# One weight buffer more in a decoder trunk on one core: three 2 MB loads fewer, and an expert ring of eight rows, then of ten

## What is computed

```python
def peer(h, wq, subkeys, u_tab, v_tab):
    q = (xt @ wq).reshape(t, PEER_HEADS, 2, PEER_HALF)
    sc = jnp.einsum('thpc,pkc->thpk', q, subkeys, preferred_element_type=jnp.float32)
    sv, si = lax.top_k(sc, PEER_TOPK)
    cand = sv[:, :, 0, :, None] + sv[:, :, 1, None, :]
    ...
    cs, cpos = lax.top_k(cand.reshape(t, PEER_HEADS, -1), PEER_TOPK)
    idx = jnp.take_along_axis(cidx.reshape(t, PEER_HEADS, -1), cpos, axis=-1)
    gate = jax.nn.softmax(cs, axis=-1)
    ...
        act = jax.nn.gelu(jnp.einsum('td,tkd->tk', xbb, u_tab[ib], preferred_element_type=jnp.float32))
        return jnp.einsum('tk,tkd->td', gb * act, v_tab[ib].astype(jnp.float32))
```

## Time and profile before

| | |
|---|---|
| time, median of 3 executions | 1553.74 us (1551.52 to 1554.93) |
| time of the profiled execution | 1553.37 us |
| its span, first to last instruction | 1551.6 us |
| TensorE busy | 71% |
| VectorE busy | 72% |
| ScalarE busy | 50% |
| GpSimd busy | 38% |
| bytes moved by DMA | 603.39 MB, 389 GB/s over the span |
| share of the 16 DMA engines: gathers, other loads | 84.8%, 11.3% |

### The profile page before, as it was taken

One profiled execution on the slowest core, in us unless ns is written; L12 is line 12 of the kernel. 1 busy time (PEld: TensorE's weight loads), 2 busy tenths in 40 slices (PEclk: granted clock), 3 DMA queues, 4 the chain that ended last, 5 costly groups with the idle time before them and its releaser, 6 DMA issues.

```text
span 1551.6 us, 19133 instructions
## 1 busy us (share of the span) xinstructions
PE 1097.8 (71%) x5920; PEld 348.4 (22%) x5920; DVE 1111.5 (72%) x2533; ACT 770.2 (50%) x2120; POOL 589.4 (38%) x517
## 2 busy tenths in 40 slices
PE   7997678866765666679866575656878666666665
PEld 3542222322211212223221121212323111111110
DVE  2356887479787899985477799999456866666554
ACT  2315554445456667764334666766334644444433
POOL 0024343323443354554334345344432443434430
PEclk9998689878966776879988567686998777676675
DMA  9569999999999998999999999999999999999995
GB/s 358 179 234 413 420 405 418 414 415 408 415 421 421 354 374 358 410 421 415 412 413 414 403 357 369 355 363 406 380 416 415 415 422 421 421 421 421 421 422 234
DMA packets 105418, 603.39 MB, mean 389 GB/s; under 512 B 9314, under 2 KB 9442, under 8 KB 39780
## 3 DMA queue, kind: packets, MB, share of 16 engines
q0 software_dynamic: 73728, 536.90, 84.8%
q1 hardware_dynamic: 31588, 65.26, 11.3%
HBM read 601.08 MB, written 1.05 MB: 388 GB/s over the span
## 4 chain that ended last, share of the span: by engine, by line
DMA 32%; DVE 31%; PE 22%; ACT 7%; issue 3%; DVEq 3%; ACTq 1%; POOL 1%; SPq 0%; POOLq 0%
DMA rings<-in_uv_tab_dram,idx 24%; DVE rings L1324 11%; PE ps L715 9%; PE ps L920 8%; DMA wst<-in_wq_dram 7%; DVE mem L1231 2%; PE ps L908 2%; DVE dgs L1324 2%; ACT dgs L667 1%; DVE mem L1213 1%; ACT wgt L664 1%; DMA rings<-in_w_in_dram 1%; DVE mem L1242 1%; ACT L661 1%; DVE mem L1240 1%
## 5 line engine op out<-in xcount | busy, mean ns | idle before, releaser
L920 PE MATMUL ps<-rings,dgs 64*64 64x512 f32 x3648 | 638.0, 804 | 343.3 <-ACT dgs L667 342.6
L463 POOL DMA_INDIRECT rings<-in_uv_tab_dram,idx x456 | 521.7, 1144 | 804.3 <-PE ps L920 687.8
L1324 DVE CUSTOM_DVE_ANT_0 rings<-rings,h 128x1024 f32<-128x1024 f32 x456 | 550.7, 1224 | 210.8 <-DMA rings<-in_uv_tab_dram,idx 197.7
L661 ACT ACTIVATE gel<-dots 128x1 f32<-128x1 f32 x512 | 102.1, 199 | 522.2 <-DVE dots L1324 518.5
L920 PEld LDWEIGHTS ps<-rings,dgs 64*64 64x64 f32 x3648 | 128.3, 163 | 783.4 <-ACT dgs L667 682.3
L667 ACT ACTIVATE dgs<-cst,wgt 128x128 f32<-128x128 f32 x512 | 205.6, 402 | 36.3 <-issue 1.5
L715 PE MATMUL ps<-wst,hT 128*128 128x512 f32 x320 | 168.0, 666 | 37.1 <-DMA wst<-in_wq_dram 20.5
L664 ACT ACTIVATE wgt<-gel,share 128x1 f32<-128x1 f32 x512 | 150.8, 295 | 35.5 <-issue 0.3
L920 PE MATMUL ps<-dgs 64*64 64x512 f32 x448 | 80.2, 795 | 53.2 <-ACT dgs L667 53.1
L463 POOL DMA_INDIRECT dgs<-in_uv_tab_dram,idx x56 | 65.9, 1176 | 88.3 <-PE ps L920 74.8
L715 PEld LDWEIGHTS ps<-wst,hT 128*128 128x128 f32 x320 | 63.4, 212 | 138.1 <-issue 134.9
(11 more groups left out here) (192 smaller groups left out, 991.2 us busy)
## 6 DMA issues: line engine op xcount, KB each, us to landing
wst<-in_wq_dram SPq DMA_DIRECT2D x15, 2048.0 KB, 28.2
wst<-in_w_out_dram SPq DMA_DIRECT2D x4, 2048.0 KB, 22.8
wst<-in_glu_w_dram SPq DMA_DIRECT2D x4, 2048.0 KB, 31.7
rings<-in_uv_tab_dram,idx POOLq DMA_INDIRECT x456, 15.7
rings<-in_w_in_dram SPq DMA_DIRECT2D x3, 2048.0 KB, 16.7
rings<-in_w_in_dram SPq DMA_DIRECT2D x2, 1024.0 KB, 7.5
dgs<-in_w_in_dram SPq DMA_DIRECT2D x1, 2048.0 KB, 19.4
vec<-in_vecs_dram SPq DMA_DIRECT2D x3, 512.0 KB, 17.2
```

Source lines behind the costliest of these rows:

```text
L463: nc.gpsimd.indirect_dma_start(out=ring[g % RING], out_offset=None, in_=uv_tab, in_offset=bass.IndirectOffsetOnAxis(ap=idx[n % AHEAD][:, s ...
L661: A.activation(gel[i][:, every], dots[i][:, every], ACT.Gelu_apprx_tanh)
L920: ins = PE.matmul(ps[64 * b:64 * b + 64, 4 + 2 * t + half, :], diag[rows, g % DIAGS, rows], ring[g % RING][rows, D + b * BANK:D + (b + 1) ...
L1324: V.tensor_tensor_reduce(out=u, in0=u, in1=h[:, t, :], scale=1.0, scalar=0.0, op0=ALU.mult, op1=ALU.add, accum_out=dots[n % 2][:, s:s + 1] ...
```

## The change

- A third weight buffer: the whole tile `dgs` (2 MB), free once block 3 of the input projection has been used for both tiles. For that (1, 3) moves ahead to the first place of tile 1 in `Z_ORDER`.
- The output projection's two blocks stay in the halves of `wst` from their use for tile 0 (uses 0 and 1) to that for tile 1 (uses 5 and 6). Query blocks 0, 1 and 2 of layer 0 pass one after the other through the third buffer; block 2 stays there until its use for tile 1 (use 9). `BLOCK_OF` names the block of each use, `BUFFER` the buffer of each block. There are 20 loads.
- The diagonals move to a tile of their own (`dia`), 7 slots instead of 16, and ScalarE waits for the row that had the slot.
- The ring has 8 slots (all in `rings`) for rows 0 to 79 and 10 from row 80 on (two more in `dgs`, once use 9 is over). The copies of indices and gates go from 16 to 8.
- The queries of tile 1 come in the order 3, 2, 0, 1, at slots 68, 74, 81, 89 instead of 3, 0, 1, 2 at 68, 76, 84, 92; the routing of groups 6 to 12 starts 4 to 6 slots later.

```diff
-RING = 9
-AHEAD = 16
+SHORT, RING = 8, 10
+SHORT_ROWS = 80
+AHEAD = 8
 PACE = 1
-DIAGS = 16
+DIAGS = 7
...
-SHARED_USE = 8
+BLOCK_OF = [0, 1, 2, 3, 4, 0, 1, 5, 5, 4, 6, 7] + list(range(8, 20))
+BUFFER = [0, 1, 2, 2, 2, 0, 1, 0] + [1, 0] * 6
...
-Z_ORDER = [(0, 0), (0, 1), (0, 2), (0, 4), (0, 3), (1, 0), (1, 1), (1, 2), (1, 4), (1, 3)]
+Z_ORDER = [(0, 0), (0, 1), (0, 2), (0, 4), (0, 3), (1, 3), (1, 0), (1, 1), (1, 2), (1, 4)]
...
             def load_w(*which):
                 for w in which:
-                    if w >= 2:
-                        last_use = w - 2 + (w - 2 >= SHARED_USE - 1)
+                    earlier = [v for v in range(w) if BUFFER[v] == BUFFER[w]]
+                    if earlier:
+                        last_use = max(u for u in range(len(BLOCK_OF)) if BLOCK_OF[u] == earlier[-1])
                         sp.wait_ge(w_used, last_use + 1)
+                    elif BUFFER[w] == 2:
+                        sp.wait_ge(z_done, Z_ORDER.index((1, 3)) + 1)
...
-                if g < RING and g % 2 == 0:
-                    pool.wait_ge(z_done, 6 + g // 2)
-                if g >= RING:
-                    pool.wait_ge(v_done, g - RING + 1)
+                if g < SHORT and g % 2 == 0:
+                    pool.wait_ge(z_done, 7 + g // 2)
+                if row_ahead(g) >= 0:
+                    pool.wait_ge(v_done, row_ahead(g) + 1)
+                elif ring_at(g) == SHORT:
+                    pool.wait_ge(w_used, Q_USE[1, 2] + 1)
...
+                if g >= DIAGS:
+                    act.wait_ge(v_done, g - DIAGS + 1)
```

More of the change, by code:

```diff
@@ L154, in between @@
         at(0, slot, (names[0],))
-    query(0, 76, 1, 0)
-    query(0, 84, 1, 1)
-    query(0, 92, 1, 2)
+    query(5, 1, 1, 0)
+    query(5, 9, 1, 1)
     for t in range(T):
@@ L272, in trunk @@
         sgb = sb("sgb", [P, 8])
-        ring = [rings[:, 2 * D * i:2 * D * (i + 1)] for i in range(8)] + [dgs[:, 2 * D:4 * D]]
+        ring = [w[:, 2 * D * i:2 * D * (i + 1)] for w, rows in ((rings, SHORT), (dgs, RING - SHORT)) for i in range(rows)]
+        weights_in = [wst[:, 0, :, :], wst[:, 1, :, :], dgs[:, :].rearrange("p (k n) -> p k n", k=KC)]
         qs = part(8448, BANK)
@@ L317, in trunk @@
         ld_win = [sem(f"ld_win{n}") for n in range(5)]
-        ld_w = [sem(f"ld_w{i}") for i in range(2)]
+        ld_w = [sem(f"ld_w{i}") for i in range(3)]
         ld_vec, ld_col, ld_row = sem("ld_vec"), sem("ld_col"), sem("ld_row")
@@ L359, in bc, with ring_at, ring_turn, row_ahead @@
             return ap.to_broadcast([ap.shape[0]] + [ap.shape[1 + at] if d is None else d for d in dims])
+        def ring_at(g):
+            return g % SHORT if g < SHORT_ROWS else (g - SHORT_ROWS) % RING
+        def ring_turn(g):
+            b = ring_at(g)
+            return sum(ring_at(r) == b for r in range(g + 1))
+        def row_ahead(g):
+            earlier = [r for r in range(g) if ring_at(r) == ring_at(g)]
+            return earlier[-1] if earlier else -1
+        def nth_in(w):
+            return sum(BUFFER[i] == BUFFER[w] for i in range(w + 1))
         def block_of(use):
-            return use - (use >= SHARED_USE)
+            return BLOCK_OF[use]
         def score_cols(p, b):
-            c = 2 * (b if p == 0 else (b + 1) % 4)
+            c = 2 * ((2, 3, 1, 0)[b] if p == 1 else b)
             return slice(c, c + 2)
@@ L562, in q_keep @@
                 if p > 0:
-                    last = cols.stop if p == 1 else PH * (p - 1) + 2 * b + 2
+                    last = {1: cols.stop, 2: 2 * PH, 3: 2 * PH + cols.stop}[p]
                     act.wait_ge(idx_ok, last)
```

50 lines of the change are left out of this document (26 added, 24 removed).

## The result

| | before | changed |
|---|---|---|
| median of 19 runs (lowest to highest) | 1553.74 us (1551.52 to 1556.14) | 1559.84 us (1555.83 to 1561.77) |
| profiled execution, own time / span | 1553.37 / 1551.6 us | 1559.49 / 1557.8 us |
| bytes moved | 603.39 MB | 597.09 MB |

The ratio is 1.0035 [1.0028, 1.0042], paired by chip: 5.4 us slower (4.4 to 6.5). The forecast of 1548.0 has the wrong sign, and 1559.8 lies above its range. In what follows a ratio is turned into microseconds with 1553.9.

The account below looks back on a forecast made before the run. The prediction took the kernel as a prelude bound by its chain of operations, then alternating DMA-bound and VectorE-bound stages. Its terms, 5.8 + 1.9 - 10.0 + 1.8 - 5.0 = -5.5 us, gave 1548 us, range 1543 to 1555.

Parts of the forecast that it names:

- late first query load, and the clock behind it: Prelude: TensorE waits for the first query block, +5.8 us, then runs at half clock, +1.9 us; nothing covers the wait.
- two loads fewer: DMA-bound windows up to 510 us: two weight loads at 4.98 us each saved, -10.0 us; bounds 0 and -11.3.
- ring of eight for 80 rows: First 80 rows: gathers go out one row's completion later, +1.8 us, priced at row 37; bounds 0 and 4.6.
- then one slot more: Ring of ten from row 80: 2.49 us gained at the end of each of two VectorE-bound stages, -5.0 us.
- its own sign: Sign of being wrong: row 128 late by more than 3 us would fault the price of the loads or ring of eight.
- theory D: Theory set up for the experiments: the loads, once gone, bring nothing.
- the slow rival: VectorE, not DMA, sets the pace of rows 16 to 96, so the -10.0 falls away: +4.5 us, 1558; chance 0.10.
- the rival's 7.1: Ring of eight costs 7.1 instead of 1.8 us: feedback at every thin place plus a further row; 1553.3, chance 0.12.
- The rest at nothing: Diagonals, second block's rotary work, and moved queries and routings cost 0; the latter were said to stay in DMA-bound windows.
- My own sign: Sign of being right: row 128 nearly unchanged (-0.5 us), then -2.5 us at the end of each VectorE-bound stage.

Follow-up runs that it names:

- e7: Kernel before, with the first query block's load held until the sixth projection product is done: 1561.49 us, ratio 1.0051, +7.9 us.
- e5: Kernel before, with the output projection load issued at 203.68 us cut to an eighth of its bytes: 1549.67 us, ratio 0.9969, -4.8 us.
- e6: Kernel before, with the load issued at 341.5 us (query block 2, tile 1) cut to an eighth of its bytes: 1551.15 us, ratio 0.9985, -2.3 us.
- e3: Kernel before, with a ring of eight for rows 0 to 79, then nine: 1558.33 us, ratio 1.0032, +5.0 us.
- e10: Kernel before, with seven diagonals in their own tile and a ring of nine to row 80, then ten: 1548.47 us, ratio 0.9972, -4.4 us.
- e8: Kernel before, with only the routing of group 12 moved from slot 120 to 126: 1559.64 us, ratio 1.0036, +5.6 us.
- e1: Changed kernel, with routings of groups 8 to 12 moved earlier, group 12 from slot 126 to 120: 1555.66 us, ratio 1.0012 to the kernel before.
- e4: Kernel before with its 23 loads, seven diagonals in their own tile and a ring of ten from the first row: 1547.94 us, ratio 0.9961, -6.1 us.

## Why the prediction was wrong

The parts, each measured by itself at the kernel before, against the term that I gave them:

| part | forecast | measured | from |
|---|---|---|---|
| late first query load, and the clock behind it | +7.7 | +7.9 | e7 |
| two loads fewer | -10.0 | -8.2 | e5 and e6, times 8/7 |
| ring of eight for 80 rows | +1.8 | +5.0 | e3 |
| then one slot more | -5.0 | -4.4 | e10 |
| the rest: routing of group 12 past row 128 | 0 | +5.6 | e8 |
| sum | -5.5 | +5.9 | the kernel itself: +5.4 |

The sum of the parts lies within the interval of the whole, 4.4 to 6.5. Each part is known to about 2 us only, and their sum to about 5, so parts that were left out, or that act on each other, by less than that would not be seen here.

The rows of the changed kernel give a second account that does not need the parts to be independent. From one execution, it is 7.7 us at the first row (forecast 7.7), then +3.8 by row 16 (the ring of eight, 1.8), -4.9 between rows 16 and 128 (the two loads, -10.0), +5.8 between 128 and 136 (nothing), and -6.3 behind (the ring of ten, -5.0). Both accounts give the step at row 128 5.6 to 5.8 us. They differ on the ring of eight and the loads: 5.0 us worse than forecast by the parts, 7.1 by the rows. So the prediction also failed ahead of row 128, as its own sign says: from the first row to row 128 the changed kernel is 1.1 us shorter and not 8.2.

1. **The prelude** was right in each step: the issue after the projection piece (77.13, forecast 77.7), 8 us to landing, a wait of 5.72, and 1.82 us for the clock. That the idle stretch at 354 us with its half clock would repeat itself here was a good reading: the same length of idle, nearly the same price. Nothing behind the first gather takes it back (e7).

2. **The loads** were right in kind: theory D and the slow rival, by which the bytes bring nothing, fall with e5. The second was mis-sized, 2.7 instead of 5. Together with what else changes up to row 128 the changed kernel shows -4.9 where I had -10.0. The window 340 to 510 us has a DMA share of 1.01 as a whole, but the stretch behind the load, rows 80 to 104, gains nothing (e6), and only half of the load's time comes out at row 112. That the work of VectorE and TensorE for tile 1's queries keeps the rest back is what the place suggests; no run took that work away, so the cause of this half stays open. The Trainium skill, DMA: Bandwidth & Descriptors, section "Where 436 GB/s comes from", puts the memory's side at about 358 GB/s; by that figure 7/8 of a load is an estimated 5.1 us, by the 421 GB/s of the trace 4.4. The 4.8 measured (3.0 to 6.7) does not decide between them, but the changed kernel's 421 GB/s over 1300 to 1500 us does, and it does not agree with that section's figure. This program runs on one core alone, and no run here had a second core at work.

3. **The ring of eight** is a term that was mis-sized. I looked at the thinnest place of the trace, row 37, and said of it that "the delay does not feed back into the next issue". The first thin place was row 15. The trace of before has its issue 1.6 us ahead of a weight load, behind a query product; I costed the first rows only up to the seventh. There the ring of eight lets row 15 out behind the product and behind the load, 3.8 us of waiting at once (e3), of which 2.9 stay, and at rows 38 to 45 the delay does feed back while the load of 206 us runs beside them. The measured 5.0 (3.0 to 6.8) lies just above my upper bound of 4.6 and below the rival's 7.1; I had taken 1.8 from row 37 alone.

4. **The ring of ten** came as forecast in size (-4.4, interval -6.1 to -2.6), but not where. I had put -2.5 at the end of each VectorE-bound stage; in e10 the first gave -2.5 at row 232, lost again at row 248 and back at row 272, and the end of the second, between rows 336 and 360, near -4.4 more, of which the end kept all but some 0.2. That is -7.0 in an execution 2.1 us faster than its median, so the places are surer than the sizes.

5. **"The rest at nothing" is the step that failed.** I wrote that "the queries and routings that move by some slots stay in DMA-bound windows". For group 12 that is false: slot 126 plus the eight slots of a routing is 134, and from row 128 on gathers do not set the pace. I had read the whole window 340 to 510 us as DMA-bound by its share of 1.01. Row 128 is taken at 478.9 us in the kernel before and row 134 at 497.1, inside that window, where the share is still 1.01 but VectorE hardly waits for gathers. My own sign spoke of row 128 as the end of the stage; my price went by the window. I checked that the indices come early enough for their rows, which is a question of lateness, and not whether VectorE has waits for gathers to spare where the work lands, which is one of price. Six slots cost 5.6 us (3.4 to 7.8), the largest cost behind the prelude's 7.9, and as much as my whole forecast gain. In place of nothing the runs show 2.9 + 2.8 us of routing work on VectorE behind row 128 (e8), and a step that is gone when the routing ends at slot 128 again (e1). None of my rivals named it; the one that ended on the slow side was another mechanism, and it was false.

Of the 11.4 us between my sum and the sum of the parts, 5.6 are this step, 3.2 the ring, 1.8 the loads, 0.6 the ring of ten and 0.2 the prelude, each by its middle value. That the prelude and the ring of ten came out near their terms did not help: without the step of group 12, the parts still add up to about no change (+0.3), not to the forecast gain.

Open stays why group 12 alone costs 5.6 at the kernel before (e8) while moving it back with four others gave 3.6 in the changed one (e1): the intervals, 3.4 to 7.8 and 1.9 to 5.4, overlap, but the two are not shown to be the same.

## What to carry to other kernels

Where a kernel is a row of stages with different bounds, list every piece of work that a change moves, with its last slot and not only its first, against the bound of the stage where it lands, and read that bound from what the engine waits for there, not from the busy share of a wide window: here six slots across a border cost 5.6 us, and moving eight routings forward, of which those of groups 13 and 19 had run behind such a border, gave 11.0 together with a ring of ten that alone gave 6.1. A buffer fewer is to be costed at the place where its release stands behind the longest product and its transfer behind a big load, not at the place where the fewest transfers are under way. And a change made of a gain and its costs is best cut apart: the longer ring alone (e4, -6.1 us) was worth more than the whole with its loads saved.
